# Two layers with a 16-expert mixture: half of each expert's gate and up weights loaded four rows to a partition, features split four apart

## The chip, the cores and the metric

The kernel is one program on one core of a Trainium2 chip. The metric is device microseconds of one execution, lower is better; a run is summed up by the median of its executions. All data are float32.

## The reference

Three blocks run one after the other on a sequence of 256 tokens with 1024 features: two layers of a three-branch attention block, then one layer of a second block (neighbourhood attention, a gated recurrence, and a mixture of experts). The change touches the end of the second block, the mixture, and the vectors that scale its input (written here in short):

```
h2 = modulate(rms_norm_2(x, g_pre2[l]), sh2, sc2)
x = x + gt2 * rms_norm_2(ec_moe(h2, w_router[l], w_gate[l], w_up[l], w_down[l]), g_post2[l])

def ec_moe(h, w_router, w_gate, w_up, w_down):   # cap = 32 tokens for each of 16 experts
    aff = softmax(h @ w_router); gate, idx = top_k(aff^T, cap)
    xs = h[idx]
    hid = silu(xs @ w_gate) * (xs @ w_up)            # w_gate, w_up: 1024 x 2752 each, per expert
    y = (hid @ w_down) * gate                        # w_down: 2752 x 1024
    return scatter-add of y to the tokens
```

So each expert reads 33.8 MB of weights once, for 32 tokens.

## The kernel before

**Before the mixture.** TensorE works through the first three layers' matmuls while SP's DMA queue brings weights into a ring in SBUF. In the second block's attention the work goes in ticks (a loop over `TICKS2`): ACT computes an exponential (line 2130), DVE takes its reciprocal and scales (lines 2391, 2393), and PE transposes the scaled scores (line 1951). At tick 4 ACT also issues ten DMAs (lines 2153 to 2159): two broadcasts of 512 KB, and then eight tiny loads that gather the vectors `g_pre2` and the shift and scale biases from a table, element by element, into the layout of features over partitions.

**Layout of features.** A product over 1024 features is cut into eight blocks, kt = 0 to 7, of 128 features. Before the change block kt holds every second feature of a range of 256, so that partition p has the features 2p and 2p+1 of the range in the blocks kt and kt+1. The tokens are brought to that layout by matmuls or transposes that read the token matrix with a step of two elements: line 1861 (the modulation rows), line 2091 (the residual for the router), line 2687 (`gather`, which also picks each expert's tokens by a one-hot matrix).

**The ring of the mixture.** SBUF has seven places of 5504 elements to a partition (22,016 bytes; 2752 KB over 128 partitions), `mslot` in line 1759. Places 0 and 1 lie side by side, and so do places 2 and 4. SP loads the weights in one fixed order (`MLOADS`, from `expert_loads` in line 464). For expert 0 there are eight loads "both", one for each kt, of one row of gate and one of up to a partition (two DMAs of 1376 KB). For each expert after it there are eight loads of two rows to a partition: gate 0, up 0, gate 1, up 1, gate 2, up 2, gate 3, up 3, where i covers kt = 2i and 2i+1. Each is one DMA of 2752 KB (lines 2654 and 2655). Then come five loads of down, 0 to 4: the first three of 2048 KB, number 3 with 256 KB more, and number 4 in three DMAs (lines 2636 to 2648). Load n goes to place n % 7, and SP waits before it until load n - 7 has been used (lines 2618 to 2621): `rows_used` counts finished pairs of blocks and the first three down loads, `gu_done` the end of the gate and up products, `dn_done` the end of the expert.

**PE's work for one expert** (lines 2755 to 2831). For every kt, 24 matmuls of line 2783 and four of line 2787 multiply 32 tokens by gate and up rows; in front of an even kt it waits for the two loads (`arrived`, line 2698). After kt 0 comes the scatter of the previous expert's result (line 2709), after kt 1 a small matmul that spreads ranks (line 2696):

```
if kt < 7 and (e == 0 or kt % 2 == 1):
    mm.then_inc(rows_used.sem, rows_used.up())
if kt == 0 and e > 0:
    scatter(e - 1)
if kt == 1:
    spread_ranks(e)
```

Then ACT and DVE form the hidden state in three pieces, PE transposes them (line 2752; the hidden features are read with a step of four elements in the first two pieces, and of two or one in the third), and PE multiplies by down (line 2818), one group of 16 matmuls for each of the five loads, with four closing pairs in lines 2830 and 2831. At experts 0, 4, 8 and 12 a gather for the next four experts stands ahead of kt 0.

## Time and profile before

| what | value |
|---|---|
| median of 3 runs | 2256.9 us (2253.99 to 2258.21) |
| the profiled execution | 2256.61 us, its span 2254.7 us |
| PE busy | 1773.8 us, 79% of the span |
| DMA, HBM read | 708.97 MB, mean of all traffic 317 GB/s over the span |
| chain that ended last | PE 52%, DMA 45% of the span |
| mean granted clock of TensorE | 0.886 of full speed |

The span runs from the first to the last instruction. The page cuts it into 40 slices of 56 us; DMA traffic stands at 425 GB/s or more from slice 19 (about 1015 us) to the last but one. The chain that ended last is followed back from the last instruction, at each step to what released it. DMA issues are listed by the queue of the engine that issues them (SPq, ACTq), and data of a load lands later than its issue.

### The profile page before, as it was taken

Reading aid. Unit: us, or ns where it says so; the run is one execution under the profiler, and the core shown is the slowest. Engines: PE = TensorE matmul, PEld = TensorE weight load, DVE = VectorE, ACT = ScalarE, POOL = GpSimd, SP = SyncE. Lnnn points to the kernel's source line nnn. Section 1 sums busy time; section 2 is a strip of 40 time slices with the busy share of each in tenths; the row PEclk is TensorE's granted clock in tenths of the full one; section 3 lists DMA queues with packets and bytes.
Section 4 is the critical chain, followed back from the end, with each engine's and each line's share of the span. In section 5 each row is a group of like instructions: output and inputs, shape, how many; then the busy total and the mean of one; then the engine's idle time right before and its main releaser. Section 6 shows DMA issues by size and latency. Waiting matters only on the chain.

```text
span 2254.7 us, 23457 instructions
## 1 busy us (share of the span) xinstructions
PE 1773.8 (79%) x10122; PEld 981.7 (44%) x10122; DVE 503.7 (22%) x1127; ACT 321.6 (14%) x758; POOL 51.6 (2%) x91
## 2 busy tenths in 40 slices
PE   7999999999999999997656665665765566666666
PEld 4887885887786654652212221221222122222222
DVE  3254322164223446441000010000100000000001
ACT  1224401224401123220000000000000000000001
POOL 1000000000004000100000000000000000000000
PEclk9999999999999999998878787787877878787788
DMA  9864453455454524589999999999999999999997
GB/s 325 226 233 176 161 171 112 165 206 186 160 207 131 187 58 148 188 354 425 425 430 428 427 427 428 429 425 429 429 426 428 428 427 425 430 429 426 429 429 299
DMA packets 126764, 714.28 MB, mean 317 GB/s; under 512 B 11577, under 2 KB 16249, under 8 KB 96975
## 3 DMA queue, kind: packets, MB, share of 16 engines
q1 hardware_dynamic: 118240, 698.12, 76.4%
q10 hardware_dynamic: 6151, 8.78, 1.2%
q0 software_dynamic: 2272, 5.90, 1.2%
q8 instruction: 80, 1.31, 0.2%
q14 instruction: 21, 0.17, 0.0%
HBM read 708.97 MB, written 3.80 MB: 316 GB/s over the span
## 4 chain that ended last, share of the span: by engine, by line
PE 52%; DMA 45%; SPq 1%; DVE 1%; issue 0%; ACT 0%; ACTq 0%; DVEq 0%
DMA arena<-in_w_up_dram 23%; DMA arena<-in_w_down_dram 21%; PE banks L875 15%; PE banks L2783 5%; PE banks L942 4%; PE banks L1887 2%; PE banks L1892 2%; PE banks L2818 2%; PE banks L950 2%; PE banks L1873 2%; PE banks L2830 1%; PE banks L1009 1%; DMA arena<-in_w_mods_dram 1%; PE banks L1037 1%; PE banks L962 1%; PE banks L1019 1%
## 5 line engine op out<-in xcount | busy, mean ns | idle before, releaser
L2783 PE MATMUL banks<-arena 128*32 128x512 f32 (+2 forms) x3072 | 425.2, 692 | 324.4 <-DMA arena<-in_w_up_dram 324.4
L2783 PEld LDWEIGHTS banks<-arena 128*32 128x32 f32 x3072 | 133.5, 133 | 584.0 <-issue 578.4
L875 PE MATMUL banks<-arena 128*128 128x256 f32 x1536 | 343.3, 380 | 0.0
L875 PEld LDWEIGHTS banks<-arena 128*128 128x128 f32 x1536 | 287.9, 190 | 41.8 <-issue 5.0
L2818 PE MATMUL banks<-arena 128*32 128x512 f32 x1264 | 203.9, 798 | 91.7 <-DMA arena<-in_w_down_dram 91.7
L2917 DVE SCALAR_TENSOR_TENSOR arena<-arena,banks 64x512 f32<-64x512 f32 (+1 forms) x48 | 30.5, 635 | 515.9 <-ACT arena L2840 514.9
L2840 ACT ACTIVATE arena<-banks 64x512 f32<-64x512 f32 (+1 forms) x48 | 26.7, 556 | 820.5 <-PE banks L2783 819.2
L2818 PEld LDWEIGHTS banks<-arena 128*32 128x32 f32 x1264 | 44.1, 133 | 225.7 <-DMA arena<-in_w_down_dram 126.7
L2924 DVE COPY arena<-banks 128x512 f32<-128x512 f32 x16 | 11.1, 691 | 344.5 <-PE banks L2831 325.8
L942 PE MATMUL banks<-arena 128*128 128x256 f32 x384 | 83.4, 380 | 0.0
L942 PEld LDWEIGHTS banks<-arena 128*128 128x128 f32 x384 | 72.9, 190 | 10.5 <-issue 0.8
L2910 DVE COPY arena<-banks 128x256 f32<-128x256 f32 x16 | 6.8, 425 | 261.9 <-PE banks L2696 261.9
L1873 PE MATMUL banks<-arena 128*128 128x512 f32 x128 | 58.3, 601 | 0.0
L1887 PE MATMUL banks<-arena 128*128 128x256 f32 x256 | 56.7, 380 | 0.9 <-DVE arena L1391 0.9
L2709 PE MATMUL banks<-arena 128*128 128x512 f32 x120 | 56.5, 614 | 0.0
L2787 PE MATMUL banks<-arena 128*32 128x128 f32 x512 | 56.2, 300 | 0.0
L950 PE MATMUL banks<-arena 128*128 128x512 f32 x128 | 55.6, 592 | 0.0
L1892 PE MATMUL banks<-arena 128*128 128x512 f32 x128 | 55.4, 593 | 0.0
L2854 ACT COPY arena<-banks 128x512 f32<-128x512 f32 x16 | 9.4, 585 | 322.2 <-PE banks L2831 305.0
L2752 PE MATMUL banks<-arena 64*128 64x64 f32 x176 | 30.2, 289 | 31.1 <-DVE arena L2919 31.1
L1887 PEld LDWEIGHTS banks<-arena 128*128 128x128 f32 x256 | 48.2, 190 | 8.3 <-DVE arena L1391 1.1
L1235 ACT ACTIVATE arena<-arena 128x256 f32<-128x256 f32 x64 | 31.9, 500 | 113.7 <-DVE arena L1547 68.2
(362 smaller groups left out, 1712.3 us busy)
## 6 DMA issues: line engine op xcount, KB each, us to landing
arena<-in_w_gate_dram SPq DMA_DIRECT2D x60, 2752.0 KB, 35.9
arena<-in_w_up_dram SPq DMA_DIRECT2D x60, 2752.0 KB, 32.8
arena<-in_w_down_dram SPq DMA_DIRECT2D x64, 2048.0 KB, 31.2
arena<-in_w_in_dram SPq DMA_DIRECT2D x68, 1024.0 KB, 7.9
arena<-in_w_mods_dram SPq DMA_DIRECT2D x48, 1024.0 KB, 7.5
arena<-in_w_down_dram SPq DMA_DIRECT2D x31, 1024.0 KB, 27.1
arena<-in_w_out_dram SPq DMA_DIRECT2D x12, 1024.0 KB, 5.1
arena<-in_w_gate_dram SPq DMA_DIRECT2D x8, 1376.0 KB, 10.7
```

The source lines that it names most:

```text
L875: mm = pe.matmul(b[:, i * S:i * S + S], w, rhs[:, kt, :], start=kt == 0, stop=kt == 7)
L942: mm = pe.matmul(b[:, i * S:i * S + S], w[:, k, c:c + P], zv[:, 4 * br + k, :], start=k == 0, stop=k == 3)
L950: mm = pe.matmul(b, hTv[:, kt, t * P:t * P + P], slot(loads[0] + kt // 4)[:, kt % 4, :], start=kt == 0, stop=kt == 7)
L1235: ins = nc.scalar.activation(Ev[:, u % 3, t * S:t * S + S], src, ACT.Exp, bias=nmx[:, u % 3, t:t + 1], scale=QK ** -0.5 if kind == "mla" e ...
L1873: mm = pe.matmul(view(b, 2, S), slot(loads[kt // 4])[:, kt % 4, n * P:n * P + P], hbT[:, kt, :, :], start=kt == 0, stop=kt == 7)
L1887: mm = pe.matmul(b[:, i * S:i * S + S], slot(loads[kt // 4])[:, kt % 4, c0:c0 + P], rhs[:, kt, :], start=kt == 0, stop=kt == 7)
L1892: mm = pe.matmul(b, lhs[:, kt, (n % 2) * P:(n % 2) * P + P], slot(loads[kt // 4])[:, kt % 4, :], start=kt == 0, stop=kt == 7)
L2709: mm = pe.matmul(acc[2 * t + c], GT[:, e % 2, t * P:t * P + P], Y[:, 512 * c:512 * c + 512], start=e == 0, stop=False, skip_group_check=True)
L2783: mm = pe.matmul(bank[pc][32 * g:32 * g + 32, 0:w_], xsT[:, kt, CAP * e4:CAP * e4 + CAP], (wg if g < 2 else wu)[:, c:c + w_], start=kt == ...
L2787: mm = pe.matmul(bank[pc][32 * g:32 * g + 32, LAST - c0:w], xsT[:, kt, CAP * e4:CAP * e4 + CAP], (wg if g < 2 else wu)[:, FF - 64:FF].unsq ...
L2818: mm = pe.matmul(bank[c][32 * g:32 * g + 32, :], hTv3[:, j, 32 * hf:32 * hf + 32], w_[:, 512 * c:512 * c + 512], start=(g, c) not in start ...
L2917: nc.vector.scalar_tensor_tensor(h_, h_, 1.0, bank[pc][0:64, 0:w], ALU.add, ALU.mult).then_inc(own3.sem, own3.up())
```

## The change

From expert 1 on, gate and up rows 0 to 511 (kt 0 to 3) are each loaded by one DMA of four rows to a partition, 44,032 bytes, into two neighbouring places: gate 0 into places 0 and 1, up 0 into 2 and 4. Rows 512 to 1023 are still loaded by two DMAs of two rows to a partition for each matrix, now named 2 and 3 (kt 4, 5 and kt 6, 7). The expert then has six gate and up DMAs instead of eight. Up 3 and down 0 to 2 have fixed places (0, 1, 2, 4), the other five loads of an expert go round the places 6, 3, 5. SP's waits follow from a new table `RELEASED`: what last lay in the place or places. PE waits for gate 0 and up 0 ahead of kt 0, for the 2s ahead of kt 4, for the 3s ahead of kt 6, and counts `rows_used` after kt 3 and kt 5.

Features are split four apart everywhere in this part: the token matrix is read with a step of four elements (lines 1861, 2091, 2687), expert 0's loads take every fourth row of 512, the router's weights come in two blocks of four rows, and the vector loads of ACT at tick 4 become one DMA from `b_mod_2` (runs of four elements) and eight of 32 partitions with four elements each.

```diff
+PAIRS = ((0, 1), (2, 4))
+ALONE = (6, 3, 5)
...
+    rows = 7
     for e in range(NE):
-        for n in range(8):
-            loads.append((e, "both", n) if e == 0 else (e, ("gate", "up")[n % 2], n // 2))
-            done = n < 7 if e == 0 else n < 6
-            if done and (e == 0 or n % 2 == 0):
-                rows += 1
-            used.append(("rows", rows) if done else ("gate_up", 3 * e + 3))
+        if e > 0:
+            for i, user in ((0, ("rows", rows + 1)), (2, ("rows", rows + 2)), (3, ("gate_up", 3 * e + 3))):
+                for kind in ("gate", "up"):
+                    loads.append((e, kind, i))
+                    used.append(user)
+            rows += 2
         for n in range(5):
             loads.append((e, "down", n))
             rows += n < 3
             used.append(("rows", rows) if n < 3 else ("down", e + 1))
-    return loads, used
+    for n, (e, kind, i) in enumerate(loads):
+        if e == 0:
+            places.append((n % MRING,))
+        elif i == 0 and kind != "down":
+            places.append(PAIRS[kind == "up"])
+        elif (kind, i) in FIXED:
+            places.append((FIXED[kind, i],))
+        else:
+            places.append((ALONE[alone % 3],))
+            alone += 1
+    return loads, used, places
+
+
+FIXED = {("up", 3): 0, ("down", 0): 1, ("down", 1): 2, ("down", 2): 4}
+
+
+def releases(used, places):
+
+    last, out = {}, []
+    for n, at_ in enumerate(places):
+        out.append(sorted({used[last[p]] for p in at_ if p in last}))
+        for p in at_:
+            last[p] = n
+    return out
...
+FIRST_ROW = {0: 0, 2: 4, 3: 6}
 DOWN_PARTS = (1, 1, 1, 2, 3)
-MLOADS, USED = expert_loads()
+MLOADS, USED, MPLACE = expert_loads()
+RELEASED = releases(USED, MPLACE)
...
+        mpair = {0: at(a0, 2 * MROW), 2: at(b2 + 3678, 2 * MROW)}
...
-                        c = 512 * hf + i // 2 * 2 * P + i % 2
-                        mm = pe.transpose((*SB, *OT)[2 * t + hf][:, i * P:i * P + P], xv[:, t, c:c + 2 * P - 1:2], ident)
+                        c = 512 * hf + i
+                        mm = pe.transpose((*SB, *OT)[2 * t + hf][:, i * P:i * P + P], xv[:, t, c:c + 4 * P - 3:4], ident)
...
-                    for a, b in ((VV["gpre2"][0], VV["gpre2"][1]), (VV["bsh2"][0], VV["bsc2"][1])):
-                        for hf in range(2):
-                            for j in range(2):
-                                src = A["vecs"][:, a:b].rearrange("(p j) (b h) -> h j p b", j=2, h=2)[hf, j]
-                                act.dma_start(vv[64 * hf:64 * hf + 64, a + j:b:2], src, allow_slow_non_contiguous=True).then_inc(vec2_in, 16)
+                    a, b = VV["bsh2"][0], VV["bsc2"][1]
+                    act.dma_start(view(vv[:, a:b], 4, 4),
+                                  A["b_mod_2"][0, 3 * D:5 * D].rearrange("(h p k) -> p h k", h=4, k=4)).then_inc(vec2_in, 16)
+                    a, b = VV["gpre2"]
+                    for r in range(4):
+                        for h in range(2):
+                            src = A["vecs"][:, a + 4 * h + r].rearrange("(p k) -> p k", k=4)
+                            act.dma_start(vv[32 * r:32 * r + 32, a + 4 * h:a + 4 * h + 4], src,
+                                          allow_slow_non_contiguous=True).then_inc(vec2_in, 16)
...
-                        act.dma_start(view(mrow[:, 512:640], 4, 2 * NE), A["w_router_2"][0].rearrange("(b p j) e -> p b (j e)", p=P, j=2)).then_inc(wr_in, 16)
+                        act.dma_start(view(mrow[:, 512:640], 2, 4 * NE), A["w_router_2"][0].rearrange("(b p j) e -> p b (j e)", p=P, j=4)).then_inc(wr_in, 16)
...
-                    reader_of, count_of = USED[n - MRING]
-                    used = {"rows": rows_used, "gate_up": gu_done, "down": dn_done}[reader_of]
-                    sp.wait_ge(used.sem, used.at(0, count_of))
-                s_ = n % MRING
+                    for reader_of, count_of in RELEASED[n]:
+                        used = {"rows": rows_used, "gate_up": gu_done, "down": dn_done}[reader_of]
+                        sp.wait_ge(used.sem, used.at(0, count_of))
+                s_ = MPLACE[n][0]
...
-                        src = A[name][0, e, 2 * P * (i // 2):2 * P * (i // 2) + 2 * P, :].rearrange("(p k) c -> k p c", k=2)[i % 2]
+                        src = A[name][0, e, 4 * P * (i // 4):4 * P * (i // 4) + 4 * P, :].rearrange("(p k) c -> k p c", k=4)[i % 4]
                         sp.dma_start(mslot[s_][:, FF * k:FF * k + FF], src).then_inc(moe_full[s_], 16)
                 else:
-                    src = A["w_gate_2" if kind == "gate" else "w_up_2"][0, e, 2 * P * i:2 * P * i + 2 * P, :]
-                    sp.dma_start(mslot[s_], src.rearrange("(p k) c -> p (k c)", k=2)).then_inc(moe_full[s_], 16)
+                    w_ = A["w_gate_2" if kind == "gate" else "w_up_2"][0, e]
+                    if i == 0:
+                        sp.dma_start(mpair[s_], w_[0:4 * P, :].rearrange("(p k) c -> p (k c)", k=4)).then_inc(moe_full[s_], 16)
+                    else:
+                        src = w_[4 * P:8 * P, :].rearrange("(p j k) c -> j p (k c)", j=2, k=2)[i - 2]
+                        sp.dma_start(mslot[s_], src).then_inc(moe_full[s_], 16)
 
...
-                            c = kt // 2 * 2 * P + kt % 2
-                            mm = pe.matmul(to[:, k * P:k * P + P], xnv[:, t, c:c + 2 * P - 1:2],
+                            c = kt // 4 * 4 * P + kt % 4
+                            mm = pe.matmul(to[:, k * P:k * P + P], xnv[:, t, c:c + 4 * P - 3:4],
...
+                s_ = MPLACE[n][0]
+                pe.wait_ge(moe_full[s_], FULL[n])
+                return mpair[s_] if len(MPLACE[n]) == 2 else mslot[s_]
...
-                    elif kt % 2 == 0:
-                        pairs = arrived(e, "gate", kt // 2), arrived(e, "up", kt // 2)
+                    elif kt in FIRST_ROW.values():
+                        i = [n for n in FIRST_ROW if FIRST_ROW[n] <= kt][-1]
+                        pairs = arrived(e, "gate", i), arrived(e, "up", i)
                     if e > 0:
-                        wg, wu = (w_[:, FF * (kt % 2):FF * (kt % 2) + FF] for w_ in pairs)
+                        c = FF * (kt - FIRST_ROW[i])
+                        wg, wu = (w_[:, c:c + FF] for w_ in pairs)
...
-                    if kt < 7 and (e == 0 or kt % 2 == 1):
+                    if kt < 7 and (e == 0 or kt in (3, 5)):
```

SP's queue, expert 2 to expert 3, the issues in order; `arena` is SBUF, the shape is partitions by elements, and in brackets is what it waits for. Before:

```order
L2655 DMA arena<-in_w_gate_dram 128x5504 [waits gate_up_done]
L2655 DMA arena<-in_w_up_dram 128x5504 [waits gate_up_done]
L2655 DMA arena<-in_w_gate_dram 128x5504 [waits weight_rows_used]
L2655 DMA arena<-in_w_up_dram 128x5504 [waits weight_rows_used]
L2655 DMA arena<-in_w_gate_dram 128x5504 [waits weight_rows_used]
L2655 DMA arena<-in_w_up_dram 128x5504 [waits down_done]
L2655 DMA arena<-in_w_gate_dram 128x5504 [waits down_done]
L2655 DMA arena<-in_w_up_dram 128x5504 [waits weight_rows_used]
L2638 DMA arena<-in_w_down_dram 128x4096 [waits weight_rows_used] x4
```

and now:

```order
L2694 DMA arena<-in_w_gate_dram 128x11008 [waits weight_rows_used,gate_up_done]
L2694 DMA arena<-in_w_up_dram 128x11008 [waits weight_rows_used]
L2697 DMA arena<-in_w_gate_dram 128x5504 [waits gate_up_done]
L2697 DMA arena<-in_w_up_dram 128x5504 [waits down_done]
L2697 DMA arena<-in_w_gate_dram 128x5504 [waits down_done]
L2697 DMA arena<-in_w_up_dram 128x5504 [waits weight_rows_used]
L2676 DMA arena<-in_w_down_dram 128x4096 [waits weight_rows_used] x4
```

Two loads of 128x11008 stand where four of 128x5504 stood. The wait of the last up load on `weight_rows_used` (up 3) has stayed, but the count that it waits for is now that of kt 3, where it was that of kt 1.

ACT's queue at tick 4, the DMAs between two exponentials. Before:

```order
L2148 ACTIVATE arena<-banks 128x256
L2153 DMA arena<-in_b_mod_dram 128x1024
L2154 DMA arena<-in_g_post_2_dram 128x1024
L2159 DMA arena<-in_vecs_dram 64x4x1 x4
L2159 DMA arena<-in_vecs_dram 64x8x1 x4
L2130 ACTIVATE arena<-arena 128x512
```

and now:

```order
L2182 ACTIVATE arena<-banks 128x256
L2187 DMA arena<-in_b_mod_dram 128x1024
L2188 DMA arena<-in_g_post_2_dram 128x1024
L2190 DMA arena<-in_b_mod_dram 128x4x4
L2196 DMA arena<-in_vecs_dram 32x4x1 x8
L2164 ACTIVATE arena<-arena 128x512
```

Eight tiny loads, four of 64x4 and four of 64x8 single elements, have become one of 128x4 runs of four and eight of 32x4 single elements.

## Rows read from the trace of the kernel before

**Rows 1.** the page's 40 slices: GB/s moved; its chain that ended last, shares of the span.
```profile
GB/s 325 226 233 176 161 171 112 165 206 186 160 207 131 187 58 148 188 354 425 425 430 428 427 427 428 429 425 429 429 426 428 428 427 425 430 429 426 429 429 299
...
PE 52%; DMA 45%; SPq 1%; DVE 1%; issue 0%; ACT 0%; ACTq 0%; DVEq 0%
```

**Rows 2.** timeline of PE, start and length in us, matmuls of experts 2 to 4.
```profile
1142.36 4.59 PE L2783 MATMUL banks<-arena 128*32 128x512 f32 x24 [7.88 <-DMA arena<-in_w_up_dram]
...
1153.01 1.12 PE L2696 MATMUL banks<-arena 16*128 16x512 f32 x2
1155.45 2.56 PE L2783 MATMUL banks<-arena 128*32 128x512 f32 x24 [1.31 <-DMA arena<-in_w_up_dram]
...
1157.81 2.57 PE L2783 MATMUL banks<-arena 128*32 128x512 f32 x24
...
1181.67 4.91 PE L2783 MATMUL banks<-arena 128*32 128x512 f32 x24 [5.61 <-DMA arena<-in_w_up_dram]
...
1189.06 0.39 PE L2787 MATMUL banks<-arena 128*32 128x128 f32 x4
...
1208.08 3.51 PE L2818 MATMUL banks<-arena 128*32 128x512 f32 x16 [4.33 <-DMA arena<-in_w_down_dram]
...
1221.27 4.39 PE L2783 MATMUL banks<-arena 128*32 128x512 f32 x24 [7.96 <-DMA arena<-in_w_up_dram]
...
1301.54 2.56 PE L2783 MATMUL banks<-arena 128*32 128x512 f32 x24 [2.36 <-DMA arena<-in_w_up_dram]
```

**Rows 3.** DMA view of the stretch 1050 to 2200 us.
```profile
DMA packets 33209, 491.93 MB, mean 428 GB/s; under 512 B 3685, under 2 KB 3685, under 8 KB 7269
...
q8 instruction: 39, 0.64, 0.2%
```

**Rows 4.** DMA view of the stretch 816.5 to 818.5 us.
```profile
DMA packets 1533, 0.01 MB, mean 3 GB/s; under 512 B 1533, under 2 KB 1533, under 8 KB 1533
...
q10 hardware_dynamic: 1533, 0.01, 40.2%
```

**Rows 5.** timeline of SP's DMA queue, the issues that wait for kt 1, experts 2 and 4.
```profile
1153.17 0.33 SPq L2655 DMA_DIRECT2D arena<-in_w_up_dram  x1
...
1310.34 0.33 SPq L2655 DMA_DIRECT2D arena<-in_w_up_dram  x1
```

**Rows 6.** stretches of expert 2's first burst: busy us per engine, PEclk, DMA share, GB/s.
```profile
1142.36:1146.50 4.14, 4.14 (x24) 1.28 (x26) 0.00 (x0) 0.00 (x0) 0.00 (x0) 0.50 1.02 435
1146.50:1153.09 6.59, 6.59 (x47) 2.56 (x39) 0.00 (x0) 0.00 (x0) 0.00 (x0) 1.00 1.00 428
```

**Rows 7.** SP's issue of a load with an empty queue, and GB/s in half microseconds after it.
```profile
1013.27 0.33 SPq L2652 DMA_DIRECT2D arena<-in_w_gate_dram  x1
...
1013.50:1014.00 0.50, 0.50 (x6) 0.50 (x6) 0.00 (x0) 0.00 (x0) 0.00 (x0) 1.00 0.00 0
1014.00:1014.50 0.50, 0.50 (x6) 0.50 (x6) 0.14 (x1) 0.00 (x0) 0.00 (x0) 1.00 1.77 297
```

**Rows 8.** ACT's queue and PE around 810 us; the chain's row there; line 2159's issues.
```profile
809.87 0.46 ACTq L2154 DMA_DIRECT2D arena<-in_g_post_dram  x1
...
810.36 7.31 ACTq L2159 DMA_DIRECT2D arena<-in_vecs_dram  x8
...
819.31 1.12 PE L1951 MATMUL banks<-arena 128*128 128x128 f32 x4 [3.80 <-DVE arena L2393]
...
810.36 2.59 ACTq L2159
...
L2159 ACTq DMA_DIRECT2D arena<-in_vecs_dram x8: 627/648/2592, 810.4 to 817.0; - x8
```

**Rows 9.** weight loads of hidden-state transposes (steps of four and two); the chain's first gather.
```profile
1109.64 0.56 PEld L2752 LDWEIGHTS banks<-arena 64*128 64x128 f32 x4 [0.91 <-DVE arena L2919]
...
1112.30 0.42 PEld L2752 LDWEIGHTS banks<-arena 64*128 64x128 f32 x3 [0.66 <-DVE arena L2919]
...
1008.52 2.15 PE banks L2687 x16
```

More of the change, by code:

```diff
@@ L461 @@
 FOURTH, HALVES = [(2 * n, 2 * n + 1) for n in range(4)], [tuple(range(4 * n, 4 * n + 4)) for n in range(2)]
+PAIRS = ((0, 1), (2, 4))
+ALONE = (6, 3, 5)
 def expert_loads():
-    loads, used = [], []
-    rows = 0
-    for e in range(NE):
-        for n in range(8):
-            loads.append((e, "both", n) if e == 0 else (e, ("gate", "up")[n % 2], n // 2))
-            done = n < 7 if e == 0 else n < 6
-            if done and (e == 0 or n % 2 == 0):
-                rows += 1
-            used.append(("rows", rows) if done else ("gate_up", 3 * e + 3))
+    loads, used, places = [], [], []
+    rows = alone = 0
+    for n in range(8):
+        loads.append((0, "both", n))
+        used.append(("rows", n + 1) if n < 7 else ("gate_up", 3))
+    rows = 7
+    for e in range(NE):
+        if e > 0:
[4 more added lines that the diff above has]
+            rows += 2
         for n in range(5):
@@ L478, in expert_loads @@
             used.append(("rows", rows) if n < 3 else ("down", e + 1))
-    return loads, used
+    for n, (e, kind, i) in enumerate(loads):
[17 more added lines that the diff above has]
+    return out
 def slots_full(loads):
     total, full = [0] * MRING, []
-    for n, (_, kind, i) in enumerate(loads):
-        total[n % MRING] += 16 * PARTS(loads[n][0], kind, i)
-        full.append(total[n % MRING])
+    for n, (e, kind, i) in enumerate(loads):
+        total[MPLACE[n][0]] += 16 * PARTS(e, kind, i)
+        full.append(total[MPLACE[n][0]])
     return full
@@ L1859, in job @@
                     for i in range(4):
-                        c = 512 * (n % 2) + i // 2 * 2 * P + i % 2
-                        mm = pe.transpose(b[:, i * P:i * P + P], mrow3[:, c:c + 2 * P - 1:2], ident)
+                        c = 512 * (n % 2) + i
+                        mm = pe.transpose(b[:, i * P:i * P + P], mrow3[:, c:c + 4 * P - 3:4], ident)
                 elif kind in ("gate2", "gate3"):
@@ L2488, in _ @@
             dve.wait_ge(reader(L2, JOB2["modT2", 3]), taken(L2, JOB2["modT2", 3]))
-            dve.wait_ge(vec2_in, 128)
+            dve.wait_ge(vec2_in, 144)
             nc.vector.tensor_tensor(AB2[:, 0:8], mcv[:, 0:8, 1], V("bsh2"), ALU.add)
@@ L2699, in arrived @@
                 n = MLOAD_OF[e, kind, i]
-                pe.wait_ge(moe_full[n % MRING], FULL[n])
-                return mslot[n % MRING]
+                s_ = MPLACE[n][0]
+                pe.wait_ge(moe_full[s_], FULL[n])
+                return mpair[s_] if len(MPLACE[n]) == 2 else mslot[s_]
             def scatter(e):
```

## The prediction

> **What bounds the kernel now.** I read the page's slices first, then the chain, then single stretches. From about 1015 us to the end DMA traffic stands at 425 to 430 GB/s, the last slice apart, and the chain that ended last is PE for 52% of the span and DMA for 45% [rows 1]. So there are two halves: until the mixture begins PE sets the pace, and from then on the stream of expert weights does. PE's own timeline shows the second half in detail. In expert 2, kt 0 starts at 1142.36 when up 0 has landed, kt 2 at 1155.45, kt 6 at 1181.67, the last down group at 1208.08, and kt 0 of the next expert at 1221.27. Each of those starts ended a wait for a DMA [rows 2]. Six loads of 2752 KB take 1181.67 - 1142.36 = 39.31 us, 6.55 us each; five down loads take 26.41; an expert takes 78.9 us. What can shorten the run in this half is a faster stream, and what can lengthen it is a gap in the stream, or something late at its two ends.
>
> **Part 1: fewer, longer descriptors (a gain of about 2 us).** In 1050 to 2200 us the DMA view counts 33209 packets for 491.93 MB [rows 3]. The loads in that stretch, one packet per partition plus 16 small ones per DMA, give just that number, so I take it that a packet is a whole partition row of 22,016 bytes, and that nothing cuts it. On one of 16 engines (8 partitions) a pair of gate and up loads is 16 packets with 352,256 bytes in 13.10 us; the five down loads are 64 packets with twice the bytes in 26.41 us [rows 2]. Twice 13.10 is 26.20, so 32 more packets cost 0.21 us, some 6 ns each. The other bound is a packet with next to nothing in it: in 816.5 to 818.5 us, 1533 packets of single elements kept 16 engines busy for 40.2% of 2 us, which is 12.9 us or 8.4 ns each [rows 4]. The change takes 16 data packets and two closing ones from each engine and expert. 18 packets at 6 to 8.4 ns are 0.11 to 0.15 us, and over 15 experts 1.6 to 2.3 us. I take 2.0. The low end of this term is 0, if the hardware cuts a row of 44,032 bytes in two.
>
> **Part 2: the ring (no cost, by a margin of about 2 us per expert).** Up 3 now lies in place 0, where the first half of gate 0 was, so SP may issue it only when kt 3 is done; until then the stream lives on the three loads that are already in the queue, gate 2, up 2 and gate 3, for 3 x 6.55 = 19.7 us after up 0 has landed. Behind up 3 in SP's queue stand down 0 to 2, which wait for the same count. Against that stands PE's first burst. In expert 2 SP issued the load that waits for kt 1 at 1153.17, which is 10.8 us after kt 0 began; at expert 4, where a gather had run just before, at 1310.34, 8.8 us after 1301.54 [rows 2, 5]. The difference is the clock: PEclk was 0.50 for the first 4.14 us of the burst of expert 2, after some 8 us of idle, and 1.00 after them [rows 6], that is 1.2 and then 2.4 GHz. Now kt 2 and kt 3 follow without a wait: the rank spreading adds about 0.9 (from the row of 1.12, which overlaps the next work), and the two blocks ran from 1155.45 to 1160.38, 4.9 us [rows 2]. That makes 10.8 + 5.8 = 16.6 us. From SP's issue to the first data of an empty queue it takes about 1 us (issue at 1013.27, nothing until 1014.00, traffic in the next half microsecond) [rows 7]. 17.6 against 19.7 leaves 2.1 us. The slowest burst of two blocks in these rows lasted from 1181.67 to 1189.45, 7.8 us against 4.9 at full clock [rows 2]. With 2.9 us for the slow clock instead of 2.0 the margin is still 1.2. PE will idle longer ahead of kt 0 than now, about 8 + 13 us, so I count the slow clock at every expert, the gather's four too.
>
> The other waits have more room. Gate 0 needs up 3's place (end of kt 7) and down 0's, both free before the last two down loads have gone out; up 0 needs down 1 and 2, gate 2 the end of kt 7, up 2 and gate 3 the end of the expert before, and their turn comes 26 us and more after that. At expert 0 the order of the loads stays. The tail stays as well: the last expert's gate 3, up 3 and down loads are issued and used as before. That PE starts an expert 13 us later costs nothing as long as kt 3 is done before up 2 and gate 3 have landed, since the last wait ahead of the down products is still that for up 3.
>
> **Part 3: ACT's small loads (a cost of about 0.6 us).** At 810.36 ACT's queue starts the eight loads of line 2159, which hold it for 7.31 us: one issue of 2592 ns, the others of 627 to 657, and the exponential of the tick stands behind them. The chain goes through here, and PE idles 3.80 us until 819.31 [rows 8]. Nothing covers this. Now there are nine such DMAs. One more at 0.65 us adds 0.65. The bounds: if the new ones, with 128 elements instead of 256 and 512, are issued like the plain load of line 2154, in 0.46, the nine take 2.6 + 8 x 0.46 = 6.3, a gain of 1.0; if a second issue is held up like the first, the cost is 2.6. I take +0.6, as the issues of 64x4 and of 64x8 elements differ by less than 0.03 us, so that their length seems not to come from the elements.
>
> **Part 4: reading four elements apart (nothing).** The gather at the start of the mixture, twice 16 matmuls of 2.15 us, and the router's transposes are on the chain before the stream is. The rows have such a read already. The hidden state is transposed with a step of four elements in its first pieces, four weight loads in 0.56 us, and with two or one in the last, three in 0.42: 0.14 us each in both [rows 9]. The token matrix too is the operand that is loaded as weights, so I put this at 0. The Trainium skill (SBUF — State Buffer, section "Door 1: The DMA port swizzle", in its note on cachelines) speaks against the change here: it says that a line of 16 bytes must be hit at least twice for full speed, and a step of four float32 elements hits each line once. By that rule the gather and the transposes would become slower; the trace does not agree, since 0.14 us stands for both steps.
>
> **The sum.** The profiled execution took 2256.61 us. 2256.6 - 2.0 + 0.6 = 2255.2 us. The median of the runs, 2256.9, is 0.3 above it, which I leave aside. The terms' bounds, -2.3 to 0 and -1.0 to +2.6, give 2253.3 to 2259.2. A measurement of this kernel can tell about 0.2%, or 4.5 us, from no change, so this is the same time.
>
> **The rivals.**
>
> The room runs out (slower). If PE's first burst lasts longer than 18.7 us (19.7 less 1.0 for the issue), the stream stops at every expert. For it: the burst is my sum of pieces that ran apart, and the idle time ahead of it is one that the trace has nowhere in this half. Against it: PEclk rose after 4.14 us, and 2.1 us are left. Price: at 0.5 us over, 15 x 0.5 = 7.5 us. A second loss would come with it. One expert in three now lasts 80.3 us instead of 78.9 (1221.27 to 1301.54) [rows 2], and 39 instruction packets share the engines [rows 3]; I read this as one engine that falls behind while the others run ahead. If the others stop at every expert, the delays of different engines add up: 1.4 us at all 15 experts instead of 5, 14 us more. Together 2255.2 + 21 = about 2276 us. Chance 0.12.
>
> Strided reads cost (slower). If weight loads with a step of four took twice as long, the gather would add 4.3 us, and the router's 16 transposes, at the gather's 0.13 each, 2.1: with rounding 2261.5. Rows 9 speak against it. Chance 0.04.
>
> A row of 44,032 bytes is cut (the change does not do what it says). Then part 1 is 0 and the time 2257.2. For it: no packet of the trace is longer than 22,016 bytes. Chance 0.07.
>
> Long rows stream better than the packet count says (faster). A row read in one piece could save more than a packet's fixed time. If each doubled load gave back 0.33 us instead of 0.07, and ACT's issues took the short 0.46, the time is 2256.6 - 9.9 - 1.0 = 2245.7; with half of that gain, 2250.7. Against it: packets of 2 to 22 KB in the down and the gate loads differ by no more than the 6 ns. By the Trainium skill (DMA: Bandwidth & Descriptors, "Where 436 GB/s comes from") the sixteen ports carry 435.2 GB/s, and 5,636,096 bytes could not take less than 12.95 us there where they take 13.10, so that the whole gain would be at most 30 x 0.15 = 4.5 us, an estimate from that page, 2252.7 with part 3. Chance 0.09.
>
> **How the numbers follow.** The forecast has 0.68. With the cut rows (0.07) it makes 0.75 for a change within 0.2%. The two slower cases make 0.12 + 0.04 = 0.16, the faster one 0.09. The range takes in the bounds of the forecast, the cut rows, the strided reads and the nearer end of the faster case: 2250.7 to 2263.0; the room that runs out is left outside.
>
> **What would show it.** Right: the DMA view of the same stretch counts some 4,200 packets fewer; the distance from one expert's kt 0 to the next is 78.8; SP's issue of up 3 comes 16 to 18 us after kt 0 began, and GB/s has no dip some 20 us after kt 0; line 2130's exponential at tick 4 comes about 0.6 later. Wrong: a shorter stretch than 13.0 us for a doubled load; a period of 79.5 us and more with idle DMA ahead of up 3; matmuls of the gather 0.2 us apart instead of 0.13.

## The result, and the profile after

The changed kernel takes 2268.1 us (median of 4 runs, 2267.95 to 2268.47), the kernel before 2256.7 (4 runs, 2253.99 to 2258.21): a ratio of 1.0054, 95% interval 1.0041 to 1.0068. It is slower by 11.5 us. The forecast of 2255.2 and its range up to 2263.0 are both missed. It was the first rival that happened, in a milder form than I had priced it.

| | before | after |
|---|---|---|
| span of the profiled execution | 2254.7 | 2266.6 |
| its own time | 2256.61 | 2268.47 |
| start of the first gather | 1008.52 | 1007.75 |
| last down wait of expert 0 | 1050.12 | 1054.60 |
| last down wait of expert 15 | 2235.17 | 2248.65 |

The last three rows cut the difference of the spans, 11.9 us, into four pieces: -0.8 before the gather, +5.2 from the gather to the last down wait of expert 0 (41.60 before, 46.85 now), +9.0 over the stream of the experts (1185.05 before, 1194.05 now), and -1.6 behind it. The last piece is mostly PE's clock: the last down group took 3.54 us before, at PEclk 0.52, and 1.92 now, at 1.00.

The page of the changed kernel, where rows 1 stood for the one before: GB/s of the 40 slices, the DMA queue of the weights, and the chain's shares.

```profile
GB/s 332 232 216 186 164 156 124 150 214 177 186 198 117 180 95 110 190 368 420 415 422 429 419 422 430 428 416 424 430 414 421 430 417 421 419 430 424 414 432 333
...
q1 hardware_dynamic: 113920, 698.11, 75.9%
...
PE 63%; DMA 33%; DVE 3%; ACT 1%; issue 1%; ACTq 0%; SPq 0%; DVEq 0%; POOL 0%
```

In the mixture, where the slices before stood at 425 to 430, more than half are now at 424 or less, down to 414. The bytes are the same, so the stream has gaps. PE's share of the chain has grown from 52% to 63%: at some places transfers now wait for PE, as the timeline of PE in experts 1 to 3 shows.

```profile
1054.60 3.32 PE L2863 MATMUL banks<-arena 128*32 128x512 f32 x16 [4.31 <-DMA arena<-in_w_down_dram]
...
1080.74 4.92 PE L2828 MATMUL banks<-arena 128*32 128x512 f32 x24 [20.82 <-DMA arena<-in_w_up_dram]
...
1160.54 4.36 PE L2828 MATMUL banks<-arena 128*32 128x512 f32 x24 [19.60 <-DMA arena<-in_w_up_dram]
...
1164.84 3.70 PE L2752 MATMUL banks<-arena 128*128 128x512 f32 x8
...
1174.41 2.54 PE L2828 MATMUL banks<-arena 128*32 128x512 f32 x24
...
1188.01 4.28 PE L2828 MATMUL banks<-arena 128*32 128x512 f32 x24 [6.31 <-DMA arena<-in_w_up_dram]
...
1240.57 4.92 PE L2828 MATMUL banks<-arena 128*32 128x512 f32 x24 [20.82 <-DMA arena<-in_w_up_dram]
```

The rows of experts 1 to 3 answer to [rows 2]. The distance between the first and the last kt 0 of experts 1 to 15 (1080.74 and 2201.36) is 80.04 us per expert; before, it was 79.41 (not the 78.9 of a single expert, from which the forecast took its 78.8). PE idles about 20 us ahead of kt 0, where it idled 8. And kt 0 to 3 now follow each other without a wait, with the scatter of the expert before (L2752, 3.70) between kt 0 and kt 1.

SP's queue issues up 3 when kt 3 is done (two of fifteen such rows); behind it the stretches of expert 3 in PE's order, which starts at 1240.57, with busy us per engine, PEclk, DMA share and GB/s.

```profile
1177.05 0.33 SPq L2697 DMA_DIRECT2D arena<-in_w_up_dram  x1
...
1257.97 0.33 SPq L2697 DMA_DIRECT2D arena<-in_w_up_dram  x1
```

```profile
1256.57:1257.57 1.00, 1.00 (x18) 0.56 (x14) 0.00 (x0) 0.00 (x0) 0.00 (x0) 1.00 0.88 374
1257.57:1258.57 1.00, 1.00 (x19) 0.42 (x16) 0.00 (x0) 0.00 (x0) 0.00 (x0) 1.00 0.21 88
1258.57:1259.57 1.00, 1.00 (x16) 0.40 (x12) 0.00 (x0) 0.00 (x0) 0.00 (x0) 1.00 1.41 352
```

Up 3 goes out 16.5 and 17.4 us after kt 0 began. In the second case the stream had already fallen to 88 GB/s in the microsecond around the issue: few of the queued packets were still to start, though the forecast gave the engines work until 19.7 us.

The gather, where rows 9 stood, on the chain of the changed kernel, with the block behind it, and its weight loads from 1007 to 1020 us.

```profile
1007.75 4.10 PE banks L2729 x16
1011.85 3.48 PE banks L2828 x21
...
1015.44 3.93 PE banks L2729 x16
```

```profile
L2729 PEld LDWEIGHTS banks<-arena 128*128 128x128 f32 x32 | 7.6, 328 | 0.9 <-DVE arena L2938 0.7 <-issue 0.2
```

The same group before read as follows, in the same view and window of the kernel before.

```profile
L2687 PEld LDWEIGHTS banks<-arena 128*128 128x128 f32 x32 | 3.9, 196 | 0.9 <-DVE arena L2893 0.7 <-issue 0.2
```

A weight load of 128x128 takes 328 ns with a step of four elements, 196 with a step of two. Each of the two gathers grew by 1.9 us, from 2.15 to 4.10 and 4.00 in PE's timeline.

### The profile page after: what moved, and what is told of

Read it like the earlier page. It is cut to its first block, busy times and chain, and to the rows that moved or that the text cites. A ratio compares the mean times of both kernels' runs of the same rounds, so it can differ in the third digit from the quotient of the medians.

```text
span 2266.6 us, 23443 instructions
## 1 busy us (share of the span) xinstructions
PE 1741.1 (77%) x10122; PEld 982.8 (43%) x10122; DVE 503.9 (22%) x1127; ACT 321.6 (14%) x758; POOL 51.6 (2%) x91
## 3 DMA queue, kind: packets, MB, share of 16 engines
q1 hardware_dynamic: 113920, 698.11, 75.9%
## 4 chain that ended last, share of the span: by engine, by line
PE 63%; DMA 33%; DVE 3%; ACT 1%; issue 1%; ACTq 0%; SPq 0%; DVEq 0%; POOL 0%
DMA arena<-in_w_up_dram 28%; PE banks L908 15%; PE banks L2828 12%; PE banks L2863 4%; PE banks L975 4%; DMA arena<-in_w_down_dram 3%; PE banks L2752 2%; PE banks L1921 2%; PE banks L1926 2%; PE banks L983 2%; PE banks L1907 2%; PE banks L1042 1%; DVE arena L2964 1%; DMA arena<-in_w_mods_dram 1%; DVE arena L2962 1%; PE banks L1070 1%
## 5 line engine op out<-in xcount | busy, mean ns | idle before, releaser
L2828 PE MATMUL banks<-arena 128*32 128x512 f32 (+2 forms) x3072 | 379.1, 630 | 367.7 <-DMA arena<-in_w_up_dram 367.7
L2828 PEld LDWEIGHTS banks<-arena 128*32 128x32 f32 x3072 | 123.6, 124 | 598.8 <-issue 598.5
L2863 PEld LDWEIGHTS banks<-arena 128*32 128x32 f32 x1264 | 43.8, 132 | 227.4 <-DMA arena<-in_w_down_dram 128.8
L2752 PE MATMUL banks<-arena 128*128 128x512 f32 x120 | 57.2, 620 | 0.0
```

What stands on the lines that cost most here:

```text
L2752: mm = pe.matmul(acc[2 * t + c], GT[:, e % 2, t * P:t * P + P], Y[:, 512 * c:512 * c + 512], start=e == 0, stop=False, skip_group_check=True)
L2828: mm = pe.matmul(bank[pc][32 * g:32 * g + 32, 0:w_], xsT[:, kt, CAP * e4:CAP * e4 + CAP], (wg if g < 2 else wu)[:, c:c + w_], start=kt == ...
L2863: mm = pe.matmul(bank[c][32 * g:32 * g + 32, :], hTv3[:, j, 32 * hf:32 * hf + 32], w_[:, 512 * c:512 * c + 512], start=(g, c) not in start ...
```

## The experiments

Three theories stood to be tested. A: up 3's place comes free too late, so the stream runs dry at each expert. B: rows of 44 KB themselves cost something in the stream. C: the gather's strided weight load is what grew the head. All times below are medians, with ratios to the kernel before as it ran beside them. "Stream" is the time from expert 0's last down wait to expert 15's in the profiled execution (1185.05 before, 1194.05 in the changed kernel), and "room used" the mean time from kt 0's start to SP's issue of up 3.

**a_scatter.** The scatter goes ahead of kt 0, into PE's idle time.

```
-                    if kt == 0 and e > 0:
-                        scatter(e - 1)
+                if e > 0:
+                    scatter(e - 1)
                 for kt in range(8):
```

> The changed kernel with the scatter of the expert before (3.7 to 4.1 us) put ahead of kt 0, where PE waits for the doubled loads anyway, so that kt 3 ends some 3.7 us sooner after kt 0's start. Theory A, the place of up 3 comes free too late: up 3 is then issued about 13 us after up 0's landing instead of 16.5 to 17.7, with over 4 us of queued data left; the period of an expert falls from 80.04 us to 79.4 or less, and the kernel takes 7 to 9 us less than the changed one, about 2260. Theory B, rows of 44 KB themselves cost bandwidth or delay what is queued behind them: the period stays at 80.0 and the time within 1 us of 2268. The head of the mixture stays 5.2 us longer than before by either.

2257.4 us, ratio 1.0006 (0.9997 to 1.0015). The room used falls from 16.86 to 13.05 us, the stream from 1194.05 to 1182.86. SP's issue in a_scatter, and the stretches of PE's expert that starts at 1159.83:

```profile
1159.83 4.06 PE L2830 MATMUL banks<-arena 128*32 128x512 f32 x24 [15.23 <-DMA arena<-in_w_up_dram]
```

```profile
1172.26 0.33 SPq L2697 DMA_DIRECT2D arena<-in_w_up_dram  x1
```

```profile
1174.83:1175.83 1.00, 1.00 (x23) 0.63 (x16) 0.00 (x0) 0.00 (x0) 0.00 (x0) 1.00 0.82 352
1175.83:1176.83 1.00, 1.00 (x16) 0.39 (x12) 0.00 (x0) 0.00 (x0) 0.00 (x0) 1.00 1.08 462
1176.83:1177.83 1.00, 1.00 (x16) 0.41 (x8) 0.00 (x0) 0.00 (x0) 0.00 (x0) 1.00 1.10 457
```

Up 3 is out 12.4 us after kt 0, and 17 us after it, where the changed kernel fell to 88 GB/s, the stream goes on. In the stream 11.2 us came back, and in the medians 10.8, more than the 7 to 9 that I expected, because this stream is also 2.2 us shorter than the one before the change. For A, against B.

**a_slow2.** Two fillers in front of the rank spreading of experts 1 to 15, in the changed kernel.

```
                     pe.wait_ge(ht_ready.sem, ht_ready.at(0, 3 * e))
+                    turn_over(pe, MB, 2)
                 pe.matmul(MB, ident[0:NE, e:e + 1]...
```

> The changed kernel with two fillers (matmuls 128x512 into a bank that is read again only after them, 0.62 to 0.64 us each) between kt 1 and kt 2 of experts 1 to 14, so that kt 3 ends 1.25 us later. PE waits at the next load in either kernel, so the fillers cost nothing by themselves. Theory A: up 3 is issued 1.25 us later still, with all queues already at or near empty, so the period grows by 1.0 to 1.25 us and the kernel by 14 to 18 us, to about 2284. Theory B: no change, 2268 within 1 us.

2296.7 us, ratio 1.0189 (1.0175 to 1.0203). I had sized the fillers wrongly: the two took 1.98 us, not 1.25, since one float32 matmul of 512 columns is two such instructions here.

```profile
1172.78 1.98 PE L791 MATMUL banks<-arena 128*128 128x512 f32 x4
```

The room used is 18.79 us, 1.93 more than in the changed kernel, and the stream 1221.23, which is 27.2 more over 15 experts, 1.81 each. So an added microsecond costs nearly a whole one (1.81 for 1.93), at every expert. (In the expectations I divided such differences by 14; there are 15 bursts.) Its stretches, with kt 0 at 1162.25 and SP's issue at 1180.77, show the queue running dry in detail:

```profile
1178.25:1179.25 1.00, 1.00 (x16) 0.29 (x11) 0.00 (x0) 0.00 (x0) 0.00 (x0) 1.00 0.98 418
1179.25:1180.25 1.00, 1.00 (x16) 0.44 (x11) 0.00 (x0) 0.00 (x0) 0.00 (x0) 1.00 0.23 82
1180.25:1181.25 1.00, 1.00 (x19) 0.52 (x14) 0.00 (x0) 0.00 (x0) 0.00 (x0) 1.00 0.10 44
1181.25:1182.25 1.00, 1.00 (x16) 0.32 (x12) 0.00 (x0) 0.00 (x0) 0.00 (x0) 1.00 1.38 308
```

In this view, which counts a packet where it starts, full traffic ends 17.0 us after kt 0's start; after that the three queued loads, 19.7 us long, keep only 82 and 44 GB/s going in the next two microseconds. The times of single packets and landings in the same trace show why. Averaged over the 15 experts, up 0's last packet ends 0.6 us before kt 0 starts and gate 3's last one 19.1 us after it: together the 19.7. But that is the slowest engine. All sixteen are busy only until 16.8, ten at 17.4 and three at 18.0. They don't finish a load together: of the sixteen landings that the semaphore counts for up 0, the first comes 2.0 us before kt 0's start, the ninth 1.8, and only the last, for which kt 0 waits, 0.1.

**a_sc_slow4.** a_scatter with `turn_over(pe, MB, 4)` at the place of the fillers above.

> a_scatter with four fillers between kt 1 and kt 2: kt 3 ends 15.5 us after kt 0's start, between a_scatter's 13.0 and the changed kernel's 16.8. If there is an edge at about 16 us, where the queues run empty, the time is a_scatter's 2257.4 or up to 2 us above it; if the loss grows in proportion from 13.0 on, it takes 7 us more, about 2264.5.

2268.6 us, ratio 1.0058 (1.0045 to 1.0070): neither of the two expected values. The cause is the same wrong size. The four fillers took 3.70 us in the trace, just the scatter's length, so this is not a point between the two but the changed kernel again, with fillers in place of the scatter: room used 16.71, stream 1196.47. As a control it is worth more than what I had planned. The scatter put aside gave 11 us, and the same length of idle matmuls put back took all of it away.

**a_warm.** The scatter stays where it is; 24 fillers run in PE's idle time ahead of kt 0.

```
+                if e > 0:
+                    turn_over(pe, bank[2], 24)
                 for kt in range(8):
```

> The changed kernel, the scatter where it stands in it, with 24 fillers (matmuls 128x512 into the third bank) in front of kt 0 of experts 1 to 15, in the 20 us in which PE waits for up 0, so that kt 0 starts on a clock of 2.4 GHz instead of 1.2. Theory A, only the length of kt 0 to 3 counts, not what it is made of: kt 0 takes 2.6 us instead of 4.4, kt 3 ends 14.8 to 15 us after kt 0's start instead of 16.8; by the three kernels that I have (13.0 us: 0 lost; 16.8: 0.8 an expert; 18.8: 2.7 an expert) little is left of the loss, 0 to 0.3 an expert, so 2257 to 2261. Rival B, it was the scatter's place as such: 2268 within 2 us. If the fillers last longer than the wait, kt 0 starts late in every expert, and the time goes above 2268.

2290.2 us, ratio 1.0155 (1.0141 to 1.0169): the third case, that the fillers outlast the wait, at three experts. The PE timeline at expert 4, the stretches there, and SP's issue of up 3:

```profile
1299.96 7.70 PE L2729 MATMUL banks<-arena 128*128 128x128 f32 x32 [0.78 <-ACT arena L2901]
1309.12 22.40 PE L791 MATMUL banks<-arena 128*128 128x512 f32 x48 [1.46 <-DVE arena L2951]
1331.45 2.56 PE L2830 MATMUL banks<-arena 128*32 128x512 f32 x24
```

```profile
1336.00:1338.00 2.00, 2.00 (x8) 0.54 (x10) 0.00 (x0) 0.00 (x0) 0.00 (x0) 1.00 0.26 110
1338.00:1340.00 2.00, 2.00 (x28) 0.77 (x20) 0.00 (x0) 0.00 (x0) 0.00 (x0) 1.00 0.00 0
1340.00:1342.00 2.00, 2.00 (x16) 0.58 (x14) 0.65 (x2) 0.00 (x0) 0.00 (x0) 1.00 0.00 0
1342.00:1344.00 2.00, 2.00 (x32) 0.99 (x28) 0.26 (x1) 0.00 (x0) 0.00 (x0) 1.00 0.00 0
1344.00:1346.00 2.00, 2.00 (x32) 1.01 (x28) 0.00 (x0) 0.00 (x0) 0.00 (x0) 1.00 0.03 8
```

```profile
1346.16 0.33 SPq L2697 DMA_DIRECT2D arena<-in_w_up_dram  x1
```

At experts 4, 8 and 12 a gather of 7.70 us precedes the fillers, kt 0 starts some 11 us late, and the DMA traffic stands still for about 8 us. From one expert's last landing to the next, those three lasted 90.4, 91.2 and 87.9 us. The eleven others of the first fourteen lasted 78.7 to 80.3, like a_scatter's; of these, at expert 2, kt 0 took 2.56 us, and SP's issue came at 1175.66, 14.7 us after kt 0 at 1160.95. So a shorter burst also helps with the scatter in place, but as a whole this version is a loss, and I take only the eleven experts as evidence for A.

Put together, with the loss per expert against a_scatter's stream:

| kernel | room used, us | stream | loss per expert |
|---|---|---|---|
| a_scatter | 13.05 | 1182.86 | 0 |
| a_sc_slow4 | 16.71 | 1196.47 | 0.91 |
| changed kernel | 16.86 | 1194.05 | 0.75 |
| a_slow2 | 18.79 | 1221.23 | 2.56 |

The loss is the difference to a_scatter's stream over 15. From the last two rows back along their own slope, 1.81 per 1.93, the loss begins at about 16.1 us; a_sc_slow4 lies 0.3 above that line. Idle engines are most of the loss, not all: by the durations of its packets, an average engine idles 8.3 us longer in the changed kernel's stream than in a_scatter's, where 11.2 are lost, and 32.1 us longer in a_slow2's, where 38.4 are lost. What the rest is no run shows.

**a_split and a_split_sc.** Each doubled load as two transfers of 22 KB rows into the same places, in the changed kernel and in a_scatter.

```
-                        sp.dma_start(mpair[s_], w_[0:4 * P, :].rearrange("(p k) c -> p (k c)", k=4))...
+                        for h in range(2):
+                            sp.dma_start(mpair[s_][:, MROW * h:MROW * h + MROW],
+                                         w_[0:4 * P, :].rearrange("(p h k) c -> h p (k c)", h=2, k=2)[h])...
```

> The changed kernel with each doubled load issued as two transfers of rows of 22 KB into the same pair of places; when places come free and what is read from them is as in the changed kernel. Theory A: the period stays at 80.0 us, and the time at 2268 or up to 2 us above it for the lost longer rows (14 experts x 0.14 us). Theory B, the 44 KB rows are what costs: the period is 79.4 again and the time about 2259 to 2260.

> a_scatter with each doubled load issued as two transfers of rows of 22 KB. With the empty queues gone, what is left between this and a_scatter is the length of the rows: by the prediction's first part 0.13 to 0.16 us per expert, so 1.8 to 2.3 us over a_scatter, about 2259.5; by the rival that long rows gain nothing, 2257.4.

a_split: 2272.2 us, ratio 1.0077 (1.0063 to 1.0090), stream 1196.20. a_split_sc: 2259.9, ratio 1.0019 (1.0010 to 1.0028), stream 1185.03. Without the long rows both are slower than their partners, by 4 to 5 us (ratios 1.0077 and 1.0054) and by 2.5, so B falls. For a_split I had expected at most 2: its stream is 2.2 us longer and begins 0.7 later, and the rest of the 4 to 5 stays open. These two are also a second pair for theory A: with rows of 22 KB the scatter ahead of kt 0 gives 11.2 us of stream, the same as with rows of 44 KB. In the clean pair the long rows are worth 2.2 us of stream, and a_split_sc's stream is within 0.02 us that of the kernel before: shorter burst, same rows, same stream.

**a_gather2 and b_gather4.** The gather reads two elements apart in the changed kernel, and four apart in the one before; tokens and weight rows then no longer match in their features.

```
-                            c = kt // 4 * 4 * P + kt % 4
-                            mm = pe.matmul(to[:, k * P:k * P + P], xnv[:, t, c:c + 4 * P - 3:4],
+                            c = kt // 2 * 2 * P + kt % 2
+                            mm = pe.matmul(to[:, k * P:k * P + P], xnv[:, t, c:c + 2 * P - 1:2],
```

> The changed kernel with the gather's matmuls reading their weights two elements apart, as before, instead of four; the tokens' features then meet the wrong weight rows, and nothing else is altered. Theory C, the strided weight load is what grew the head: the first two gathers take 2.15 us each again instead of 4.10 and 4.00, kt 0 starts 1.9 us sooner and expert 0 ends 4 to 5 us sooner, so the kernel takes 4 to 5 us less, about 2264. Rival: the head is longer for the loads of expert 0, which go on under the gathers, and then the time stays at 2268 though the gathers are short.

> The kernel before with the gather's weights read four elements apart (the tokens' features then meet the wrong weight rows). Nothing else of the change is in it. Theory C: each of the first two gathers takes 4.0 to 4.1 us instead of 2.15, and from the first gather to expert 0's last down load it takes 3.3 to 5.3 us more than before's 41.6: 2259 to 2261. Rival: the price in the changed kernel comes from the clock or from its other loads, and 2256 is left.

b_gather4: 2259.4 us, ratio 1.0016 (1.0007 to 1.0025), 3.7 us for this one edit. Its timeline of PE has about the changed kernel's times, also for kt 0 behind the gather, which I hadn't counted:

```profile
1008.25 4.10 PE L2687 MATMUL banks<-arena 128*128 128x128 f32 x16 [0.58 <-DVE arena L2893]
1012.28 3.52 PE L2783 MATMUL banks<-arena 128*32 128x512 f32 x24
...
1015.74 4.00 PE L2687 MATMUL banks<-arena 128*128 128x128 f32 x16
```

Kt 0 took 2.56 before; PEclk was 0.69 over it here and 1.00 there. From the gather to expert 0's last down wait it took 44.96 us against 41.60. a_gather2 gives a mixed answer: 2266.8 us, ratio 1.0055 (1.0042 to 1.0067). The head is as short as before again (1009.70 to 1051.26, 41.56), but its stream was 1195.73, 1.7 us longer than the changed kernel's. The total moved by only 1.4 us in the medians, and not at all in the ratios (1.0054 for the changed kernel), where 4 to 5 had been expected. That a shift of its start moves the loss in a stream that runs dry is a guess; no run shows it. For the head theory C holds in every profile: the stretch lasts 41.6 to 41.8 us in the six kernels whose gather reads one or two elements apart, 44.9 to 45.2 in five of those with a step of four, and 46.7 to 47.0 in the other three, the changed kernel among them. What chooses between these two values stays open. Where the stream doesn't run dry, the gain also arrives in the total: a_best2 (below) takes 3.6 us less than a_scatter.

**a_best.** Both costs taken away: a_scatter, and ACT writes the scaled tokens in the order of the blocks, so that the gather reads a row.

```
-                nc.scalar.activation(xnv[:, t, :], xv[:, t, :], ACT.Copy, scale=...)
+                nc.scalar.activation(xnv[:, t, :].rearrange("p (b k j) -> p b k j", b=2, k=4),
+                                     xv[:, t, :].rearrange("p (b j k) -> p b k j", b=2, k=4), ACT.Copy, scale=...)
...
-                            c = kt // 4 * 4 * P + kt % 4
-                            mm = pe.matmul(to[:, k * P:k * P + P], xnv[:, t, c:c + 4 * P - 3:4],
+                            mm = pe.matmul(to[:, k * P:k * P + P], xnv[:, t, kt * P:kt * P + P],
```

> The changed kernel with both costs taken away: the scatter ahead of kt 0 as in a_scatter, and ACT writing the scaled tokens to xn in the order of the blocks (it reads four elements apart), so that the gather's weights lie in a row. If the two costs are separate and whole, it takes a_scatter's 2257.4 us less the 3.3 us by which expert 0 ended sooner in a_gather2, about 2254: 1 to 3 us below before. If ACT's scaling reads four apart at a price, that shows between the last square and the gather, and the gain is smaller by it. Rival, that the gather's cost was hidden in the whole (a_gather2 gained only 1.4 us): 2257 again.

2255.5 us, ratio 1.0000 (0.9992 to 1.0009). Gather to last down wait 41.58, stream 1182.81: both costs are gone from these two stretches. But a new one stands in front of the gather, in ACT's timeline:

```profile
999.00 2.11 ACT L2283 ACTIVATE arena<-arena 128x1024 f32<-128x1024 f32 x1 [0.56 <-POOL arena L2334]
1001.02 0.29 ACT L2290 ACTIVATE arena<-arena 128x16 f32<-128x16 f32 x1
```

The scaling takes 2.11 us instead of 1.15, and the router's last exponential, for which DVE and then the ranking wait, stands behind it.

**a_best2.** a_best with the scaling behind that exponential.

```
-            x_scaled(1)
             router_exp(1)
+            x_scaled(1)
```

> a_best with ACT's scaling of the second tile behind the second exponential of the router instead of ahead of it. In a_best the scaling, reading four elements apart, took 2.11 us instead of 1.15 and held the exponential up, for which DVE waited 1.84 us instead of 0.88; the tokens are wanted only 8 us later, at the gather. Expected: the gather starts 1.0 to 1.8 us sooner against the router's transposes, and the time is a_best's 2255.5 less that, about 2254, 1.5 below before. Rival: what follows on ACT or the head's loads set that point, and nothing is gained.

2253.8 us (11 runs, 2250.57 to 2256.35), ratio 0.9991 (0.9982 to 1.0000). Now the exponential goes first:

```profile
1000.84 0.31 ACT L2290 ACTIVATE arena<-arena 128x16 f32<-128x16 f32 x1 [1.19 <-DVE arena L2594]
...
1001.15 2.13 ACT L2283 ACTIVATE arena<-arena 128x1024 f32<-128x1024 f32 x1
```

This is the fastest kernel here: 14 us below the changed one, and 1.9 below the one before, with an interval that just reaches no difference.

**b_scatter and b_perm, controls in the kernel before.** The scatter ahead of kt 0; and the tokens written in the order of the blocks, read there two elements apart.

> The kernel before with the scatter ahead of kt 0: the control of a_scatter. In before, places come free two rows at a time and the queues never run empty. Theory A: nothing is gained by the earlier scatter, 2255.7 within 1 us. Rival, that the scatter's place is worth something for itself (by the clock or by the loads of down): some of the 10.8 us of a_scatter would show here too, 2 us or more.

> The kernel before with ACT writing the scaled tokens in the order of the blocks, so that the gather's weights lie in a row instead of two elements apart. If a read two apart costs nothing against a row, as I held of all strides in the prediction, no change, 2255.7 within 0.5 us; if the price grows with the stride from the first step on, the gathers of 2.15 us fall to under 1.9 and the kernel gains up to 1 us.

b_scatter: 2256.1 us, ratio 1.0004 (0.9995 to 1.0013), stream 1185.31. The scatter's place is worth nothing where the ring has room. b_perm: 2256.6, ratio 1.0002 (0.9993 to 1.0010); its gathers took 2.05 us instead of 2.15, and ACT's scaling 1.24 instead of 1.15. Against a step of one, a step of two cost the gather 5% and ACT's copy 8%; a step of four took 1.7 times as long in the weight load (328 for 191 ns) and 1.8 times in ACT's copy.

## Why the prediction was wrong, point by point

- **Part 1, longer descriptors: right.** -2.0 us forecast; the stream of a_scatter is 2.2 us shorter than that of a_split_sc, and the DMA queue counts 113920 packets for 118240. The row is not cut.
- **Part 2, the ring: the step that failed.** The burst was forecast well: up 3 was to be issued 16.6 us after kt 0, and it came at 16.86 on average. What failed is the other side of the comparison, that the stream lives on the queued loads "for 3 x 6.55 = 19.7 us after up 0 has landed". That is right for the slowest engine alone, counted from its own last packet, 0.6 us before kt 0 starts. Kt 0's wait ends with that engine; the others are ahead of it, and full traffic ended 17.0 us after kt 0 (a_slow2). Less the 1.0 us from issue to data, that makes the room 16.0, close to the edge that the changed kernel and a_slow2 give (16.1), and not 18.7. The margin of 2.1 us was a deficit of 0.8. Against a_scatter it cost 11.2 us over fifteen experts.
- **The rival, that the room runs out:** right mechanism, with 0.12 a small chance for what happened, and with 21 us too high a price. I had two losses in it. The first, one for one past the edge, is what a_slow2 shows; at 0.8 us over it gives 15 x 0.8 = 12 us, and 11.2 were measured. For the second, delays of different engines that add up, I had the reason for the failure in hand, "one engine that falls behind while the others run ahead", and used it for the price and not for the margin: if others run ahead, their queue is shorter than 19.7 us. At 14 us that second loss did not come. That the first alone meets the sum is in part luck, since idle engines account for 8.3 of the 11.2 us; a small second loss may be in the rest, and no run separates it.
- **Part 3, ACT's loads: right in size as far as the runs tell, but within the noise.** In the changed kernel's profile the nine issues took 6.66 us (1.43 and eight of 5.23 together), the eight before 7.31 [rows 8], which by itself would be -0.6 for +0.6. But a single profile doesn't tell: in the ten kernels with the nine issues they held the queue for 6.7 to 7.9 us, 7.4 on average, and in the four with the eight for 6.0 to 7.5, 7.0 on average. PE's idle time behind them was 3.9 and 3.4 on average. That makes +0.5, and the medians agree: a_split_sc is 4.3 us above before, less b_gather4's 3.7 that leaves 0.6, which these intervals do not tell from zero. The new issues were not as short as the plain load's 0.46: one of the first two took 1.4 to 2.6 us, and apart from it and a first one of 0.46 in three kernels they took 0.61 to 0.70. The eight matmuls after it took 6.04 us where they had taken 4.59, at a lower PEclk; over all kernels they took 3.6 to 6.1.
- **Part 4, the stride: wrong, +0 forecast, +3.7 measured.** The step that failed is reading a matmul's price from a transpose. The transposes are indeed untouched by the stride: from 825.77 to the router's first transposes at 992.88 it took 167.11 us before, from 824.97 to 992.10 after, 167.13. The weight loads of the gather's matmuls are not: 328 for 196 ns. The size that was missed is 1.9 us for each of two gathers. The Trainium skill (SBUF — State Buffer, "Door 1: The DMA port swizzle", the note on cachelines) had been set aside on the strength of the transposes. For the gather (328 for 196 ns) and for ACT (2.11 for 1.15 us) the traces now agree with it; for the transposes (212 for 211 ns) they still do not. Why they differ no run here shows. The rival's price was 4.3 + 2.1; the 4.3 was near to the 3.7 measured, and the 2.1 for transposes did not come.
- **The sum** by the measured terms: -2.2 + 3.7 + 11.2 + 0.6 = 13.3, against 11.5 measured in the medians; the terms come from separate kernels, with intervals of about 2 us each.
- **The signs** named in the forecast served: a period above 79.5 with idle DMA ahead of up 3, and a slower gather, both under "wrong", were what the trace had. The one under "right", a distance of 78.8, was no good mark: the kernel before had 79.41 on average, and a_scatter, whose stream doesn't run dry, has 79.30.

## What to carry to other kernels

When a load waits for a place that is freed late, take the room from the engine that empties first and not from the length of the queue: the wait that starts the burst ends with the slowest engine. Past that edge each further microsecond cost 0.94 per expert here. Where the room is short, work that doesn't need the loads belongs ahead of the wait for them, not between the first use and the release; where there was room, moving it gained nothing (b_scatter). And the price of a strided read is taken from the same kind of instruction: here the transposes said nothing of the gather's matmuls, nor of ACT.

## What the runs showed of the hardware

- In a queue with three loads of 2752 KB behind the one that landed, the first of the 16 engines were empty 16.8 to 17.0 us after PE's wait for that landing had ended, thirteen of them by 18.0 and the last at 19.1; between 17.0 and 19.0 the stream ran at 82 and 44 GB/s (a_slow2).
- A 128x128 float32 weight load with a step of 1, 2 and 4 elements: 191, 196 and 328 ns for the gather's matmuls (a_best, before, after); the 16 matmuls of one gather took 2.05, 2.15 and 4.0 to 4.1 us. For the router's transposes, steps of 2 and 4: 211 and 212 ns. ACT's copy of 128x1024 with its input read at steps of 1, 2 and 4: 1.15, 1.24 and 2.11 us.
- In all eight kernels whose gather reads four elements apart, the granted clock fell to 1.2 GHz late in the first gather and stayed there through most of kt 0 (from 1010.6 to 1014.0 us in the changed kernel), though PE showed as busy all the time; in none of the six others did it fall there. Kt 0 of expert 0 took 3.5 to 3.65 us instead of 2.56. The second gather, with the same step, ran at 2.4 GHz throughout (PEclk 1.00) and took 4.0 us, so its length is not the clock's. The runs show the fall with the stride and not what in it the clock answers to.
